# PEER mixers of a two-layer diffusion block: per-token gathers of expert rows replaced by dense products over all experts and a scattered table of softmax weights

## The reference

```
def one(hb):                                   # hb: 128 tokens x 1024, normed and modulated
    q = (hb @ peer_wq).reshape(128, 8, 2, 128)            # 8 heads, 2 sides
    s = einsum("thsd,hskd->thsk", q, peer_keys)           # 128 keys a side
    s_top, i_top = top_k(s, 16)
    cand = s_top[:, :, 0, :, None] + s_top[:, :, 1, None, :]
    g_score, c_idx = top_k(cand, 16)                      # 16 experts a head
    experts = e1 * 128 + e2                               # from i_top and c_idx
    gates = softmax(g_score)
    u = take(peer_u, experts)                             # 128 rows of 1024 for each token
    act = gelu(einsum("thkd,td->thk", u, hb)) * gates
    v = take(peer_v, experts)
    return einsum("thk,thkd->td", act, v)
```

## Time and profile before

| | |
|---|---|
| Time, three runs | 4393.99, 4402.45, 4402.58 us; median 4402.45 |
| Profiled execution, first to last instruction (span) | 4394.9 us |
| PE busy | 3112.4 us (71%), 12112 matrix instructions |
| DVE busy | 2859.6 us (65%) |
| POOL busy | 1584.1 us (36%) |
| ACT busy | 1122.0 us (26%) |
| Moved by DMA | 1471.78 MB, mean 335 GB/s |

### The profile page before, as it was taken

How to read it: one execution, slowest core, us unless ns; L and a number is a source line. 1 busy time by engine, 2 the same in 40 slices (tenths; PEclk the granted TensorE clock), 3 DMA queues, 4 the chain that set the end, 5 groups by cost and what they waited for, 6 DMA issues and landing times. The chain is left out here.

```text
span 4394.9 us, 37634 instructions
## 1 busy us (share of the span) xinstructions
PE 3112.4 (71%) x12112; PEld 1324.7 (30%) x12112; DVE 2859.6 (65%) x7084; ACT 1122.0 (26%) x2966; POOL 1584.1 (36%) x1383
## 2 busy tenths in 40 slices
PE   7999987676666865656666656999876755555555
PEld 4655554332222321111222112565432311111111
DVE  2524853988888897555555555665788898555554
ACT  1122531322232322111222211563332222111111
POOL 0002401545444454444444441001344455444443
PEclk9999998888887887777787887999987877777777
DMA  4114734999999999999999996103999999999998
GB/s 172 39 39 146 264 105 170 408 420 421 420 420 409 402 421 420 421 421 417 412 415 421 415 421 286 39 1 116 403 420 420 419 421 417 418 420 418 418 420 340
DMA packets 223656, 1471.78 MB, mean 335 GB/s; under 512 B 25436, under 2 KB 29244, under 8 KB 53220
## 3 DMA queue, kind: packets, MB, share of 16 engines
q0 software_dynamic: 184320, 1342.26, 73.8%
q1 hardware_dynamic: 37764, 123.17, 7.8%
q10 hardware_dynamic: 1376, 3.96, 0.2%
HBM read 1467.02 MB, written 2.28 MB: 334 GB/s over the span
## 5 line engine op out<-in xcount | busy, mean ns | idle before, releaser
L1876 PE MATMUL banks<-arena 128*64 128x512 f32 x5120 | 1672.8, 814 | 1215.1 <-ACT arena L2046 1172.1
L1678 POOL DMA_INDIRECT arena<-experts,arena x1280 | 1507.7, 1178 | 2300.9 <-PE banks L1876 1478.7
L2206 DVE CUSTOM_DVE_ANT_0 arena<-arena 128x1024 f32<-128x1024 f32 x1280 | 1535.0, 1224 | 788.7 <-DMA arena<-experts,arena 788.5
L1876 PEld LDWEIGHTS banks<-arena 128*64 128x64 f32 x5120 | 458.4, 185 | 2356.0 <-ACT arena L2046 1364.7
L2040 ACT ACTIVATE arena<-arena 128x4 f32<-128x4 f32 x320 | 66.1, 206 | 2339.7 <-DVE arena L2206 2339.6
L2046 ACT ACTIVATE arena<-arena 128x64 f32<-128x64 f32 x1280 | 340.6, 336 | 36.3
L1764 PE MATMUL banks<-arena 128*128 128x512 f32 (+3 forms) x960 | 288.5, 455 | 6.0 <-DMA arena<-wq 5.4
L434 PE MATMUL banks<-arena 128*128 128x512 f32 (+1 forms) x640 | 208.6, 486 | 1.9 <-PEq L201 1.9
L1764 PEld LDWEIGHTS banks<-arena 128*128 128x128 f32 x960 | 160.6, 191 | 112.0 <-issue 86.6
L870 POOL TENSOR_TENSOR arena<-arena 128x256 f32<-128x256 f32 x48 | 41.2, 858 | 423.6 <-POOLq L625 332.3
L1697 PE MATMUL banks<-arena 128*128 128x512 f32 x416 | 185.4, 599 | 2.3 <-PEq L953 1.5
(11 more groups left out here) (250 smaller groups left out, 2942.7 us busy)
## 6 DMA issues: line engine op xcount, KB each, us to landing
arena<-l_w_ada SPq DMA_DIRECT2D x48, 1024.0 KB, 5.0
arena<-wq SPq DMA_DIRECT2D x54, 512.0 KB, 7.9
arena<-experts,arena POOLq DMA_INDIRECT x1280, 17.1
arena<-l_w_in SPq DMA_DIRECT2D x7, 2048.0 KB, 7.9
arena<-l_w_out SPq DMA_DIRECT2D x4, 1536.0 KB, 8.8
arena<-l_w_o SPq DMA_DIRECT2D x4, 1024.0 KB, 10.0
arena<-keys SPq DMA_DIRECT2D x27, 128.0 KB, 10.4
arena<-gates SPq DMA_DIRECT2D x6, 512.0 KB, 6.5
```

Of the source, the lines that this page charges most:

```text
L1678: pool.indirect_dma_start(slots[n], None, tbl, bass.IndirectOffsetOnAxis(ap=expert[:, ring[c], k:k + 1], axis=0)).then_inc(land[n]["sem"], ...
L1876: mm = pe.matmul(core["ps"][QS * j:QS * j + QS, c, :], diag[:, g % 2, k, :], v[:, D + c * 512:D + (c + 1) * 512], start=(g % (NB * PH) == ...
L2206: dve.tensor_tensor_reduce(u, u, rep[i // PH % 2][:, k % NQ, :], 1.0, 0.0, ALU.mult, ALU.add, dots[:, k:k + 1]).then_inc(dot["sem"], up(dot))
```

## The change

The gathers, the slots, the diagonals, the dots on DVE and the spreading of rows and choices go. In their place:

- In the projection stage POOL issues 32 transfers that write zeros over two new tables in DRAM, `spread0` (16,384 experts x 768 tokens) and `spread1` (16,384 x 512), 50 MB and 34 MB.
- For each choice POOL issues 16 indirect transfers of one word per partition, which add the softmax weight into the cell (expert, token) of `spread`. Before those of head h it waits until all of the same tile's earlier heads have landed.
- `dots(b)`: PE multiplies 128 experts (block b of 128) with all tokens of the layer, 8 steps over the channels, and ACT applies the gelu to the result (`gelu(b)`); SP stores two blocks at a time to a new table `acts` in DRAM. The queries and scores of later heads lie between the blocks.
- `weigh`: after the last block, the value sums run in two passes over the tiles ((0 to 3), (4, 5) in layer 0; (0, 1), (2, 3) in layer 1). For each group of two expert blocks (64 groups a pass) SP loads the values `down` and the pass's part of `acts` and `spread`, DVE multiplies these two (`gate_acts`), and PE accumulates the tiles' sums in banks over the whole pass. The last groups of a pass run tile by tile.
- `prepare` of tiles 0 to 3 lies in layer 0's second pass; of tiles 4 and 5 in `latent_up`.

The core of the diff:

```
-            pool.indirect_dma_start(slots[n], None, tbl,
-                                    bass.IndirectOffsetOnAxis(ap=expert[:, ring[c], k:k + 1], axis=0)
-                                    ).then_inc(land[n]["sem"], up(land[n], 16))
+            for layer, width in enumerate((ZERO_W, ZERO_W * LAT // TOK)):
+                cells = d[f"spread{layer}"].rearrange("e t -> (e t)").rearrange("(j p w) -> j p w", p=P, w=width)
+                for j in range(cells.shape[0]):
+                    pool.dma_start(cells[j], d["zeros"][:, 0:width]).then_inc(cleared[layer]["sem"], up(cleared[layer], 16))
...
+            pool.wait_ge(zero["sem"], zero["base"])
+            for c, (h, t) in enumerate(order):
                 pool.wait_ge(rdy["sem"], at(rdy, c + 1))
+                if h:
+                    pool.wait_ge(spread[t]["sem"], at(spread[t], 16 * TOPK * h))
                 for k in range(TOPK):
+                    pool.indirect_dma_start(cells, bass.IndirectOffsetOnAxis(ap=expert[:, c, k:k + 1], axis=0),
+                                            gate[:, c, k:k + 1], None,
+                                            compute_op=ALU.add).then_inc(spread[t]["sem"], up(spread[t], 16))
...
+            def dots(b):
+                g, j = divmod(b, GB)
+                if j == 0:
+                    pe.wait_ge(ul[g % 4]["sem"], at(ul[g % 4], 16 * (g // 4 + 1)))
+                if b >= 2:
+                    pe.wait_ge(hev["sem"], at(hev, b - 1))
+                o = dot_pair(b)
+                for k in range(KD):
+                    for a in range(0, T, 512):
+                        z = min(a + 512, T)
+                        i = pe.matmul(o[:, a:z], us[g % 4][:, j, k, :], ht[:, k, a:z],
+                                      start=(k == 0), stop=(k == KD - 1))
+                i.then_inc(dmm["sem"], up(dmm))
+            def weigh(p, n, j, t):
+                w = hg[p][n % 4][0]
+                a = (t - passes[p][0]) * P
+                for c in range(2):
+                    i = pe.matmul(pair(core, m["pairs"][t])[:, c * 512:(c + 1) * 512], w[:, j, a:a + P],
+                                  vs[n % 4][:, j, c * 512:(c + 1) * 512],
+                                  start=(n % NG == 0 and j == 0), stop=(n % NG == NG - 1 and j == GB - 1))
+                return i
+            def arrived(n):
+                pe.wait_ge(vl[n % 4]["sem"], at(vl[n % 4], 16 * (n // 4 + 1)))
+                pe.wait_ge(am["sem"], at(am, n + 1))
...
+            for b in range(PK):
+                dots(b)
+                if b - 2 in event_at:
+                    scores(event_at[b - 2], 1)
+                if b - 1 in event_at:
+                    scores(event_at[b - 1], 0)
+                    query(event_at[b - 1], 1)
+                if b in event_at:
+                    query(event_at[b], 0)
+            for p, group in enumerate(passes):
+                for g in range(NG - tails[p]):
+                    n = p * NG + g
+                    arrived(n)
+                    for j in range(GB):
+                        for t in group:
+                            i = weigh(p, n, j, t)
+                    i.then_inc(used["sem"], up(used))
+                    for u, q in preps(n):
+                        prepare(u, q)
...
+            def load_acts(n):
+                p, g = divmod(n, NG)
+                a = passes[p][0] * P
+                if p == 0:
+                    sp.wait_ge(hst[g % 2]["sem"], at(hst[g % 2], 16 * (g // 2 + 1)))
+                for part, src in enumerate((h_d, s_d)):
+                    sp.dma_start(hg[p][n % 4][part], src[:, g * GB:(g + 1) * GB, a:a + widths[p]]
+                                 ).then_inc(hgl[n % 4]["sem"], up(hgl[n % 4], 16))
...
+            def gate_acts(n):
+                p = n // NG
+                acts, gates = hg[p][n % 4]
+                dve.wait_ge(hgl[n % 4]["sem"], at(hgl[n % 4], 32 * (n // 4 + 1)))
+                dve.tensor_tensor(flat(acts), flat(acts), flat(gates), ALU.mult).then_inc(am["sem"], up(am))
...
+     "query_at": lambda c: 2 * c - 5, "softmax_at": lambda c: 2 * c + 2,
```

More of the change, by code:

```diff
@@ L1485, in peer_block @@
     ef = take(2 * TOPK)
-    shifted = take(TOPK)
-    raised = take(TOPK)
-    total = take(2)
-    dots = take(TOPK)
-    gel = take(TOPK)
-    xg = take(2, 2 * TOPK)
-    assert top[0] <= MISC + 1400 and MISC + 1400 + 4 * P <= WORDS
+    low = take(TOPK)
+    shifted = [take(TOPK) for _ in range(2)]
+    raised = [take(TOPK) for _ in range(2)]
+    total = [take(2) for _ in range(2)]
+    assert top[0] <= WORDS
     rest = view(core, C_TRI, 2, PK)
@@ L1822, in _ @@
                 project(1, 0, K // 2, K)
+                turn_rows(0)
+                project(1, 1)
+                for t in range(2, tiles - 1):
+                    project(t, 0)
+                    turn_rows(t - 1)
+                    project(t, 1)
+                project(5, 0)
+                turn_rows(4)
+                query(0, 0)
+                query(0, 1)
+                project(5, 1)
+                scores(0, 0)
+                scores(0, 1)
+                query(1, 0)
+                query(1, 1)
+                turn_rows(5)
             else:
@@ L1912, in _ @@
+            if layer == 0:
+                up_tensor(pe, prepare)
         @block.scalar
@@ L2087, in _ @@
+            for n in range(NG, len(passes) * NG):
+                for u, p in preps(n):
                     prepare(u, p)
             if layer == 0:
-                up_scalar(act, lambda p: prepare(TT - 1, p))
+                up_scalar(act, prepare)
         @block.vector
@@ new lines, in _ @@
+                    norm_rows(t)
+            else:
+                gate_out(0, 1)
+                norm_rows(0)
+                for t in range(1, tiles):
+                    gate_out(t, 0)
+                    gate_out(t, 1)
+                    high_columns(t - 1)
+                    norm_rows(t)
+            high_columns(tiles - 1)
+            dve.wait_ge(tkl["sem"], at(tkl, 16))
+            choose_a(0)
+            for c in range(C):
+                if c + 1 < C:
+                    choose_a(c + 1)
+                choose_b(c)
@@ L2336, in _ @@
+            for p, group in enumerate(passes):
+                for g in range(2 if p else 0, NG):
+                    n = p * NG + g
+                    gate_acts(n)
+                    for u, q in preps(n):
+                        prepare(u, q)
+                if p + 1 < len(passes):
+                    for i, t in enumerate(group):
+                        add_tile(t)
+                        if i < 2:
+                            gate_acts((p + 1) * NG + i)
             if layer == 0:
@@ L2337, in _ @@
                 up_tables(dve)
-            add_tile(tiles - 1)
-            if layer == 0:
-                up_vector(dve, lambda p: prepare(TT - 1, p))
+                add_tile(4)
+                prepare(4, 1)
+                prepare(4, 3)
+                add_tile(5)
+                up_vector(dve, prepare)
+            else:
+                for t in passes[1]:
+                    add_tile(t)
     close(core)
```

897 lines of the change are left out of this document (360 added, 537 removed).

## The result

The changed kernel takes 5961.77 us, median of four runs (5960.20 to 5970.46), against 4399.87 us of the kernel before (4393.99 to 4402.58, four runs): ratio 1.356, 95% interval 1.354 to 1.358. The forecast was 5881 with a range of 5850 to 6090. It is 81 us short, and nearly all of that sits in one place. Of four runs of the changed kernel the one profiled took 5960.20 us, 1.8 us more than its span.

What follows compares the result with a forecast made beforehand. Gathers were taken to bound 3289 of 4395 us, PE mostly the rest; with dense products PE would bound: four dense terms of 4412 us plus 1,469 for all else gave 5881 us, range 5850 to 6090.

Steps and rivals of the forecast that it cites:

- Price of a dense product: Four-byte product of 512 columns on PE: two instructions, taken at 0.862 us from the input and output projections.
- The faster rival: Dense products run at a far smaller pitch; the kernel gains below 287 ns per 512-column instruction; chance 0.01.
- 3584 products: Products of 512 columns that the prediction priced at the skill's 131 ns per instruction, some 940 us.
- Zeroing: Writing 84 MB of zeros beside the projection stage: 15 us taken, bounds 0 (done by 385 us) and about 60.
- zeroing delays the scan stage more than 60 us: Rival on the stage before layer 0's dots: time about 5,990 us, chance 0.05.
- signs of being wrong: PE gap after layer 0's dots, gaps before line 1772, line 133 waiting for weights before 571 us, pitch below 431 ns.
- The forecast's own range: Whole kernel with PE at the projection's rate, everything else hidden: 5881 us, 5850 to 5960, chance 0.77.
- the rival of the value loads: Value passes bound by loads: a group takes 8 us in place of 6.9, +211, about 6,090; chance 0.09.
- Scatter: Adding transfers in layer 0's first pass: 0.938 to 1.99 us each, hidden; decides from 2.9 us; scatter-bound rival chance 0.08.
- Loads of the value passes: Two-tile value groups: loads 3.8 to 7.0 us under PE's 6.9; uncovered cost 0 to 20 us, 0 taken.
- the bound by packets (7.0): Loads of a two-tile value group: 768 packets at queue 1's mean 145 ns take 7.0 us.
- The last step, from span to time: End of the sum: 7.5 us, the earlier kernel's run median against span, takes span 5874 to 5881.

## Why the prediction was right, and where it was not

- **Price of a dense product (right).** The pitch held through 5,000 us, at 0.858 us for 512 columns (2 x 429 ns) where 0.862 was taken: dots of layer 0 1476.5 us against 1480, all value sums 2259 against 2255. The faster rival fell. The Trainium skill's 131 ns ("TensorE: Matmul & The Clock Gate", "Back-to-back issue gap") does not hold for these operands: the trace has 429 ns. The prediction said that its rows agree with that section's isolated gap of 216 ns; they don't, 431 is twice that. An instruction on two-byte operands does, at 215 ns, and it is not near 131 either. The prediction's 3584 products in that paragraph leave out the 1024 of 512 columns in layer 0's dots; the sum doesn't use the figure.
- **Zeroing (the step that failed).** The prediction gave it 15 us, with 0 and 60 as bounds, and looked for it at the modulation weights, line 133. It cost 99 us: dots at 839.6 against 741, of which 92.7 are the waits of line 439, and 4.1 the slower instructions behind them. Line 133 waited 20.0 us in the changed kernel and 20.1 before. By the prediction's own bound the term should have been 0, since the zeros were in place at 319 us, before 385. The step reasoned with mean bandwidth, "has DMA 0.11 and no need of it". The stage does need it, a little and in time: 2 MB about every 44 us. The packets' turns and not the bytes set when those arrive, as the counts of packets and the runs with 16 KB rows and with one or two transfers at a time showed. With both of its effects taken away the kernel runs in 5864.41, against 5881 - 15 = 5866 from the other terms.
- **The rivals and the range.** What happened is the rival "zeroing delays the scan stage more than 60 us", to which the prediction gave 0.05 and 5,990 us, by a path that it didn't name; none of its signs of being wrong pointed at the projection's loads. The forecast's own range ended at 5960, below the measured time. That the whole range holds it is in part luck: its top was set by the rival of the value loads, which did not occur.
- **Scatter (right, on the margin that was given).** The pitch is 1.87 us, near the upper bound 1.99 from the earlier trace rows and under the 2.9 at which it decides. Leaving it out gave nothing; doubling it to 3.74 crossed the threshold and cost over 1,100 us. DMA was forecast near 2 tenths in the dots and had 0.49: the bytes were right (94 GB/s against 88), the engines' time for the scatter's single words, 19.6%, was left out.
- **Loads of the value passes (right).** A floor of 4.07 us a group against 6.9 leaves the cover that the choice of 0 assumed; the bound by packets (7.0) was too dark.
- **Small terms, which cancel.** 7.4 us more between layer 0 and layer 1's projection, of which three waits of PE in the up projections and `prepare` (lines 1813, 1101, 1803) are 6.7, and 4 more in the last value sums; 3.5, 0.9 and 5.9 less in the dots and ahead of layer 1's; together 1 us. Within the value sums two waits of 7.2 us for gated activations, where a tail begins, stand against the lower pitch. The last step, from span to time, was 7.5 us and should have been 1.8 for the profiled run. So that the sum without zeroing comes within 2 us of 5864.41 is better than its parts deserve; by the span alone it is 5859 against 5863.8.

## What to carry to other kernels

A background transfer is not harmless because the stage beside it moves few bytes: ask how long its packets are and whether its queue ever runs empty, and let one transfer land before the next is issued, or use shorter rows. Each has its price at the issuing engine: one at a time ended the stage 41.4 us late, and rows of 2 KB 65.1 us. Before a gather is replaced by a dense product, price the product in instructions of its own type from a row of the same shape; here 4,412 us of dense work at four bytes replaced 3,289 us of gathers, and of the kernels run with the scatter only the one at two bytes was faster. When that bound moves, take the next one by its pitch in a window, not by its busy time: the scatter was free at 1.87 us under a slow PE and the bound under a fast one.

## What the runs showed of the hardware beyond what was expected

- While two queues had work, the DMA engines passed one packet of each in turn, whatever their lengths: 396 to 397 beside 64 KB packets, 831 to 834 beside 16 KB ones. A load of 1,024 rows of 2 KB, which lands in 8 us alone, took 50 us beside 16 KB packets and 130.7 us where most of its turns lay beside 64 KB ones; one of 128 KB in as many rows of 128 bytes took 154 and 160 us in place of 4.3. Two transfers in flight were as bad as 32; one was harmless.
- 32 zeroing transfers were issued in 16 us with long rows (3,328 packets), and in 358 us with 2 KB rows (20,992 packets), 328 us of them standing at issue.
- An adding indirect transfer of 128 single words keeps POOL busy 1.557 us, comes every 1.87 us and lands in 3.1 us (median), whether its target table is one or two. Some 640 of them in 1200 us took 19.6% of the DMA engines' time for 0.37 MB.
- PE ran four-byte products without a pause for 1,396 us at clock 1.00, the upper level (2.4 GHz), with DMA at 0.49. A product of 512 columns took 0.858 us at four bytes and 0.215 at two.
